# Three gated branches of a transformer block: weights made the moving operand, and the merged sum turned by TensorE

## The chip, the cores and the metric

The program runs on one core of a Trainium2 chip. The metric is the device time of one execution in microseconds (us). TensorE (PE in the profile) multiplies matrices, VectorE is DVE, ScalarE is ACT, and SyncE (SP) issues the DMAs. All engines run their own instruction streams in program order and meet through semaphores.

## The reference, cut to what matters

The first block (256 tokens, 1024 features) ends its mixer with three branches, each a matmul multiplied by a gate of its own:

```
gates = sigmoid(gate_pre)                       # [256 tokens, 3 branches, 1024]
merged = gates[0] * y_conv + gates[1] * y_sb + gates[2] * y_x
# y_conv = conv @ w_conv_out, y_sb = o_sb @ w_sb_out, y_x = o_x @ w_x_out
# gate_pre = h @ w_in[:, 7*1024:10*1024]
x = x + merged @ w_out
h2 = rms_norm(x, g_mlp)
x = x + square(relu(h2 @ w_up)) @ w_down
```

Two further layers follow. All is float32.

## The kernel before, in words

**Weights.** Every weight matrix streams in as "halves" of 1 MB, `[128, 2048]` float32, 4 tiles of 512 columns or 8 of 256. SyncE loads half `l` into `raw[:, l % 2]` once DVE has finished with half `l - 2`. ACT's `split` rounds it to `w_hi` (L331) and DVE's `split` forms the remainder `w_lo = raw - w_hi` (L725); both write slot `l % 4` of a ring of four. A product of float32 precision is three products: hi*hi, lo*hi, hi*lo. In the loop over `h` of the first block (`for h in range(FFN1)`), each engine does what belongs to half `h`, and ACT and DVE then split half `h + 4`, which may begin once PE has finished half `h` (`gemm_done`).

**Two ways to multiply.** `rows_first` (its matmuls are recorded at L1282) holds a 128x128 piece of the weights and moves 256 tokens past it: 48 matmuls of 256 columns for a half, and the result stands feature-first, `[128 features, 256 tokens]` twice in one PSUM bank. `tokens_half` and `tokens_part` (L1321, L1322, L1327) hold 128 tokens of the activation and move 512 weight columns: 24 matmuls of 512 columns for a half, and the result stands token-first, `[128 tokens, 512 features]`, in two banks, one for each `m` of the two token groups. With `tokens_half` a half is only half of the contraction, so two halves (`g` 0 and 1) make up one pair of banks.

**The stage that is changed: halves 36 to 59.** Three branches of eight halves: 36 to 43 the stick-breaking attention ("sb"), 44 to 51 the cross attention ("x"), 52 to 59 the convolution ("conv"). Even halves are gate weights, odd ones the branch's output weights, all by `rows_first`. PSUM `gps` banks 0 to 2 are used in turn; PE starts half `h` when half `h - 3` has been read out (semaphore `evac`). ACT applies the sigmoid to an even half (L557) and copies an odd one to `staged` (L347); DVE multiplies by the gate and adds into `merged` (L1073, L1075, L1077). In the last branch each quarter of `merged` is rounded to `Q_hi` by ACT (L565) and `Q_lo` is formed by DVE (L1083). They are the stationary operand of halves 60 to 63, `merged @ w_out`, by `tokens_part` into the `aps` banks. `square`, norm and MLP follow (halves 64 to 95).

**Beside it.** Cross attention is computed in the same loop iterations, 35 to 40: after the matmuls of a half PE issues `cx_values` (L1490), `cx_transpose` (L1479) and `cx_scores` (L1468) of neighbouring heads, DVE the maximum (L1010, L1013) and scaling (L1018, L1021), ACT the exponential (L511) and copies (L497, L504). The norm of the query heads takes a Ln (L351) and an Exp (L353) on ACT, and its last one (`head_rsqrt(7)`) is due in iteration 36.

Of the kernel before, what the change touches and what calls it, by code (L numbers as in the profile page):

```python
# [14 lines left out]
F32 = mybir.dt.float32  # L15
# [5 lines left out]
P = 128  # L21
D = 1024
# [52 lines left out]
def build(nc, mem_t, x_t, x, w1, w2, wf, rows1, rows2, par1, par2, con1, con2, out):  # L75
    with ExitStack() as ctx:
# [3 lines left out]
        def sem(name):  # L80
# [35 lines left out]
        merged, ox = B1, B3  # L116
# [5 lines left out]
        scaled = B1[:, :, :].rearrange("p a t -> p (a t)").rearrange("p (m n) -> p m n", m=2)  # L122
# [47 lines left out]
            mg mg_hi mg_lo ffn_relu ffn_sq ffn_hi hidden  # L170
# [152 lines left out]
        def _(act):  # L323
# [200 lines left out]
            for h in range(FFN1):  # L524
# [194 lines left out]
        def _(dve):  # L719
# [311 lines left out]
            for h in range(FFN1):  # L1031
# [34 lines left out]
                elif 36 <= h < WO1 and (h - 36) % 2 == 1:  # L1066
                    i = (h - 36) // 2 % 4
                    dve.wait_ge(s["evac"], h + 1)
                    m = merged[:, 2 * i:2 * i + 2, :]
                    sg, gg = staged[:, staged_n % 2, :], gate[:, staged_n % 2, :]  # L1070
                    staged_n += 1
                    if h < GATED["x"]:
                        dve.tensor_tensor(m, two(sg), two(gg), ALU.mult).then_inc(s["staged_free"], 1)  # L1073
                    else:
# [200 lines left out]
        def _(pe):  # L1275
# [221 lines left out]
            for h in range(FFN1):  # L1497
# [14 lines left out]
                elif h < WO1:  # L1512
                    if (h - 36) % 2 == 0:
                        rows_first(0, h, h % 3, H_hi, H_lo)
                    elif h < GATED["x"]:
                        if h == GATED["sb"] + 1:
                            pe.wait_ge(s["sb_olo"], SB_PAIRS)
# [345 lines left out]
```

## Time and profile before

| | |
|---|---|
| median of 3 runs | 1312.22 us (1306.88, 1312.22, 1312.27) |
| the profiled execution | 1308.6 us; its span, first to last instruction, 1306.8 us |
| PE busy | 1245.1 us (95% of the span) |
| PE in the chain that ended last | 75% of the span |
| halves 36 to 59 | 268.29 to 424.60 us of the span |
| halves 60 to 63 | 424.60 to 446.40 us |

Times inside the trace count from the span's start. A row of a timeline is: start, duration, engine, line, operation, what it writes and reads, shapes, how many are merged in the row (xN), and, in square brackets, how long the engine had been idle before it and what ended that. A matmul's duration contains its passage through the array, so the interval between the starts of two matmuls is what each costs in a stream.

### The profile page before, as it was taken

The numbers are of one execution on the slowest core, as the hardware profiler recorded it, in microseconds if no ns is written. First come the engines' busy times: TensorE is split into PE (matmuls) and PEld (weight loads), VectorE is DVE, ScalarE is ACT, GpSimd is POOL, SyncE is SP. The second block draws the span as 40 slices with busy tenths as digits, with TensorE's granted clock in tenths as the row PEclk, the third lists the DMA queues.
The fourth block names the chain that finished last, engine by engine and source line by source line (L and its number), as shares of the span: only waits on it lengthen the run. The fifth ranks groups of instructions, "written<-read, shape, count | busy, mean of one in ns | idle before, by whom it ended". The sixth has DMA issues, their size and how long they took to land.

```text
span 1306.8 us, 19708 instructions
## 1 busy us (share of the span) xinstructions
PE 1245.1 (95%) x8208; PEld 1124.8 (86%) x8208; DVE 775.6 (59%) x823; ACT 616.4 (47%) x676; POOL 0.2 (0%) x4
## 2 busy tenths in 40 slices
PE   5989999999999999999999989999998998899997
PEld 5979998989999899998787868989978886789896
DVE  5566875764555565555356586555566566765545
ACT  4555554664534454444254535544435434454441
POOL 0000000000000000000000000000000000000000
PEclk9989999999999999999999999999999999999999
DMA  6644344433655356554353334655525334365550
GB/s 214 219 158 162 127 164 144 179 125 134 214 203 181 129 212 207 193 183 171 114 202 108 148 139 166 222 181 199 169 94 194 129 129 177 130 209 193 193 193 32
DMA packets 33250, 216.88 MB, mean 166 GB/s; under 512 B 4384, under 2 KB 6432, under 8 KB 7456
## 3 DMA queue, kind: packets, MB, share of 16 engines
q1 hardware_dynamic: 33184, 215.92, 47.5%
q8 instruction: 51, 0.84, 0.3%
q14 instruction: 15, 0.12, 0.0%
HBM read 214.85 MB, written 1.05 MB: 165 GB/s over the span
## 4 chain that ended last, share of the span: by engine, by line
PE 75%; DVE 11%; DMA 6%; ACT 5%; issue 2%; SPq 0%; ACTq 0%; DVEq 0%
PE gps L1282 39%; PE aps L1321 7%; PE aps L1322 7%; PE aps L1327 7%; DMA raw<-w 6%; DVE w_lo L725 4%; PE gps L1321 3%; ACT w_hi L331 3%; PE gps L1322 3%; PE gps L1327 3%; PE aps L1432 1%; DVE B L873 1%; DVE rs L863 1%; DVE B L867 1%; DVE B L817 1%
## 5 line engine op out<-in xcount | busy, mean ns | idle before, releaser
L725 DVE TENSOR_TENSOR w_lo<-raw,w_hi 128x2048 fp32r<-128x2048 f32 x200 | 449.0, 2248 | 288.1 <-ACT w_hi L331 287.8
L331 ACT ACTIVATE w_hi<-raw 128x2048 fp32r<-128x2048 f32 x200 | 374.1, 1875 | 210.9 <-DMA raw<-w 122.1
L1282 PE MATMUL gps<-H_hi,w_hi 128*128 128x256 f32 x896 | 240.9, 290 | 12.5 <-ACT H_hi L366 5.7
L1282 PE MATMUL gps<-H_hi,w_lo 128*128 128x256 f32 x896 | 236.6, 285 | 0.0
L1282 PE MATMUL gps<-R_hi,w_hi 128*128 128x256 f32 x800 | 209.2, 283 | 0.0
L1282 PE MATMUL gps<-R_hi,w_lo 128*128 128x256 f32 x800 | 209.0, 283 | 0.0
L1282 PEld LDWEIGHTS gps<-H_hi,w_hi 128*128 128x128 f32 x896 | 174.1, 194 | 16.4 <-issue 12.9
L1282 PE MATMUL gps<-H_lo,w_hi 128*128 128x256 f32 x896 | 181.4, 285 | 0.0
L1282 PEld LDWEIGHTS gps<-H_hi,w_lo 128*128 128x128 f32 x896 | 174.1, 194 | 0.7 <-issue 0.5
L1321 PE MATMUL aps<-w_hi,Q_hi 128*128 128x512 f32 x416 | 162.2, 390 | 0.8 <-DVE Q_lo L923 0.8
L1322 PE MATMUL aps<-w_lo,Q_hi 128*128 128x512 f32 x416 | 162.1, 390 | 0.0
L1282 PE MATMUL gps<-R_lo,w_hi 128*128 128x256 f32 x800 | 160.5, 283 | 0.0
L1282 PEld LDWEIGHTS gps<-R_hi,w_lo 128*128 128x128 f32 x800 | 153.5, 192 | 0.8
L1282 PEld LDWEIGHTS gps<-R_hi,w_hi 128*128 128x128 f32 x800 | 153.4, 192 | 0.8
L1282 PEld LDWEIGHTS gps<-H_lo,w_hi 128*128 128x128 f32 x896 | 141.1, 194 | 0.0
L1282 PEld LDWEIGHTS gps<-R_lo,w_hi 128*128 128x128 f32 x800 | 124.5, 192 | 0.0
L1327 PE MATMUL aps<-w_hi,Q_lo 128*128 128x512 f32 x416 | 111.2, 389 | 0.0
L1321 PEld LDWEIGHTS aps<-w_hi,Q_hi 128*128 128x128 f32 x416 | 78.2, 188 | 16.5 <-DVE Q_lo L923 1.0
L1327 PEld LDWEIGHTS aps<-w_hi,Q_lo 128*128 128x128 f32 x416 | 78.1, 188 | 16.2
L1322 PEld LDWEIGHTS aps<-w_lo,Q_hi 128*128 128x128 f32 x416 | 78.2, 188 | 15.7
L406 ACT ACTIVATE staged<-gps 128x512 f32<-128x512 f32 x42 | 25.0, 596 | 103.6 <-PE gps L1282 103.6
L347 ACT ACTIVATE B<-gps 128x512 f32<-128x512 f32 x56 | 32.3, 588 | 72.2 <-PE gps L1282 63.3
(223 smaller groups left out, 1377.2 us busy)
## 6 DMA issues: line engine op xcount, KB each, us to landing
raw<-w SPq DMA_DIRECT2D x196, 1024.0 KB, 4.9
B<-rows SPq DMA_DIRECT2D x4, 1024.0 KB, 4.5
B<-x_t SPq DMA_DIRECT2D x2, 512.0 KB, 4.6
B<-mem_t SPq DMA_DIRECT2D x1, 1024.0 KB, 9.1
B<-x SPq DMA_DIRECT2D x1, 1024.0 KB, 7.7
B<-con SPq DMA_DIRECT2D x1, 1024.0 KB, 9.6
out<-B SPq DMA_DIRECT2D x4, 256.0 KB, 2.0
B<-rows SPq DMA_DIRECT2D x1, 512.0 KB, 6.2
```

The costliest lines, as they stand in the source:

```text
L331: act.activation(w_hi[:, ring(l), 0:n], raw[:, raw_slot(l), 0:n], ACT.Copy)\
L347: act.activation(dst, src, ACT.Copy, scale=scale).then_inc(s["evac"], 1)
L406: act.activation(staged[:, a, :], up_bank(par_, a), ACT.Relu)\
L725: dve.tensor_tensor(w_lo[:, ring(l), 0:n], raw[:, raw_slot(l), 0:n], w_hi[:, ring(l), 0:n].bitcast(F32), ALU.subtract)\
L817: ins = dve.scalar_tensor_tensor(t, t, scale, out, ALU.mult, ALU.add)
L863: st.mark(dve.bn_stats(stats[:, m, 6 * j:6 * j + 6], chunk(X, m, j)))
L867: st.mark(dve.scalar_tensor_tensor(t, t, stats[:, m, 12:13], g_row[:, 512 * j:512 * (j + 1)], ALU.subtract, ALU.mult))
L873: dve.scalar_tensor_tensor(t, t, stats[:, m, 17:18], b_row[:, 512 * j:512 * (j + 1)], ALU.mult, ALU.add).then_inc(s["t_z"], 1)
L1282: return pe.matmul(gps[:, bank_, nt * T:(nt + 1) * T], w[:, r, c:c + P], op[:, k, :], start=start, stop=stop, skip_group_check=True)
L1321: pe.matmul(out, x, w_hi[:, r, c], start=(start and k == ks[0]), stop=False)
L1322: pe.matmul(out, x, w_lo[:, r, c], start=False, stop=False)
L1327: ins = pe.matmul(out, op_lo[:, 4 * g + k, rows], w_hi[:, r, c], start=False, stop=(stop and k == ks[-1]))
```

## The change

The 24 halves of the stage are all multiplied token-first. They are ordered in quadruples: two halves make gate columns `512*c` to `512*c + 511` for both token groups, and two make the same columns of the branch. ACT therefore does nothing for a bank in half of the iterations and handles two banks in the others; DVE does its work for a branch once in four. `merged` lies token-first, so it has to be turned before it can be the stationary operand: PE transposes it against the identity (16 transposes of 128x128) into `aps` banks, 8 after the matmuls of half 56 and 4 after each token group's matmuls of half 60, and ACT and DVE make `Q_hi` and `Q_lo` from there. The host packs the weights in another order; their bytes and their number of DMAs stay.

```
-        merged, ox = B1, B3
+        ox = B3
...
+        merged = scaled = B1[:, :, :].rearrange("p a t -> p (a t)").rearrange("p (m n) -> p m n", m=2)
...
@@ ACT
-                    if (h - 36) % 2 == 0:
-
-                        act.wait_ge(s["gemm_done"], h + 1)
-                        act.wait_ge(s["staged_free"], staged_n - 1)
-                        act.activation(gate[:, staged_n % 2, :], ps, ACT.Sigmoid).then_inc(s["evac"], 1)
-                    else:
-                        act.wait_ge(s["staged_free"], staged_n - 1)
-                        evac(staged[:, staged_n % 2, :], ps, h + 1)
-                        staged_n += 1
-                        if h > GATED["conv"]:
-                            i = (h - GATED["conv"]) // 2
-                            act.wait_ge(s["mg"], i + 1)
-                            act.activation(Q_hi[:, 2 * i:2 * i + 2, :], merged[:, 2 * i:2 * i + 2, :],
-                                           ACT.Copy).then_inc(s["mg_hi"], 1)
+                    if (h - 36) % 4 == 1:
+                        for m in range(2):
+                            act.wait_ge(s["gemm_done"], h + 1)
+                            act.wait_ge(s["staged_free"], staged_n + m - 1)
+                            act.activation(gate[:, m, :], bank(h - 1 + m), ACT.Sigmoid).then_inc(s["evac"], 1)
+                    elif (h - 36) % 4 == 3:
+                        for m in range(2):
+                            act.wait_ge(s["staged_free"], staged_n - 1)
+                            evac(staged[:, m, :], bank(h - 1 + m), h + 1)
+                            staged_n += 1
                 elif h == WO1:
                     act.preload_act_table_set("natural_log_exp_and_others")
+                if h in (GATED["conv"] + 4, WO1):
+                    for m in range(2):
+                        j = int(h == WO1)
+                        act.wait_ge(s["mg_tr"], 2 * j + m + 1)
+                        act.activation(operand(Q_hi, m, j), four(turned(m, j)), ACT.Copy)\
+                           .then_inc(s["mg_hi"], 1)
...
@@ DVE
-                elif 36 <= h < WO1 and (h - 36) % 2 == 1:
...
+                elif 36 <= h < WO1 and (h - 36) % 4 == 3:
+                    for m in range(2):
+                        dve.wait_ge(s["evac"], h + m)
+                        t = chunk(merged, m, (h - 36) // 4 % 2)
+                        sg, gg = staged[:, m, :], gate[:, m, :]
+                        staged_n += 1
+                        if h < GATED["x"]:
+                            dve.tensor_tensor(t, sg, gg, ALU.mult).then_inc(s["staged_free"], 1)
+                        else:
+                            st.mark(dve.tensor_tensor(sg, sg, gg, ALU.mult))
+                            st.settle()
+                            dve.tensor_tensor(t, t, sg, ALU.add).then_inc(s["staged_free"], 1)
+                            if h > GATED["conv"]:
+                                dve.wait_ge(s["staged_free"], staged_n)
+                                dve.sem_inc(s["mg"], 1)
+                if h in (GATED["conv"] + 4, WO1):
+                    for m in range(2):
+                        j = int(h == WO1)
+                        dve.wait_ge(s["mg_hi"], 2 * j + m + 1)
+                        dve.tensor_tensor(operand(Q_lo, m, j), four(turned(m, j)),
+                                          operand(Q_hi, m, j).bitcast(F32), ALU.subtract)\
                            .then_inc(s["mg_lo"], 1)
...
@@ PE
+            def turn_merged(j, m):
+
+                pe.wait_ge(s["mg"], 2 * j + m + 1)
+                for k in range(4):
+                    ins = pe.transpose(turned(m, j)[:, k * P:(k + 1) * P],
+                                       chunk(merged, m, j)[:, k * P:(k + 1) * P], ident)
+                ins.then_inc(s["mg_tr"], 1)
...
-                    if (h - 36) % 2 == 0:
-                        rows_first(0, h, h % 3, H_hi, H_lo)
...
+                    g, first = (h - 36) % 2, GATED["conv"] + 2
+                    banks = ((h - g) % 3, (h - g + 1) % 3)
+                    second_free = h - 1 if g == 0 else None
+                    if (h - 36) % 4 < 2:
+                        tokens_half(0, h, g, banks, H_hi, H_lo, second_free)
...
+                    if h == GATED["conv"] + 4:
+                        turn_merged(0, 0)
+                        turn_merged(0, 1)
                 elif h < WO1 + 2:
                     pe.wait_ge(s["lo_ready"], h + 1)
                     for m in range(2):
+                        c = m + 1 if h == WO1 else m + 3
                         ins = tokens_part(h, acc(m, h - WO1), m, 0, Q_hi, Q_lo, start=True,
-                                          hi_ready=(s["mg_hi"], 2), lo_ready=(s["mg_lo"], 2))
-                    ins.then_inc(s["gemm_done"], 1)
+                                          hi_ready=(s["mg_lo"], c))
+                        if m == 1:
+                            ins.then_inc(s["gemm_done"], 1)
+                        if h == WO1:
+                            turn_merged(1, m)
...
@@ host
-        return [x[i:i + 1] for i in range(4) for x in (g, w)]
+        return [value_halves(x[:, c:c + 512]) for c in (0, 512) for x in (g, w)]
```

How the instruction order changes is shown at three places. First ACT in iterations 36 and 37, from the first head's exponential (L511) on. `ACT_TABLE_LOAD` loads the tables of another function; the line beside it is the instruction that needs it (L557 the sigmoid, L351 Ln, L353 Exp, L331 the split of a weight half, L504 and L497 copies out of cross attention). Before:

```order
L511 ACTIVATE B,small<-aps,small 128x256
L557 ACT_TABLE_LOAD [waits staged_free]
L557 ACTIVATE B<-gps 128x512 [waits gemm_done]
L331 ACTIVATE w_hi<-raw 128x2048 [waits gemm_done,raw_loaded0]
L351 ACT_TABLE_LOAD
L351 ACTIVATE rs<-rs 128x256 [waits hn_var]
L353 ACT_TABLE_LOAD
L353 ACTIVATE rs<-rs 128x256 [waits act_step]
L504 ACTIVATE B<-aps 128x512 [waits cx_t]
L511 ACTIVATE B,small<-aps,small 128x256 [waits cx_t,cx_max]
```

The same place of the changed kernel:

```order
L511 ACTIVATE B,small<-aps,small 128x256
L331 ACTIVATE w_hi<-raw 128x2048 [waits gemm_done,raw_loaded0]
L351 ACTIVATE rs<-rs 128x256 [waits hn_var]
L353 ACTIVATE rs<-rs 128x256 [waits act_step]
L504 ACTIVATE B<-aps 128x512 [waits cx_t]
L511 ACTIVATE B,small<-aps,small 128x256 [waits cx_t,cx_max]
L511 ACTIVATE B,small<-aps,small 128x256
L557 ACT_TABLE_LOAD [waits staged_free]
L557 ACTIVATE B<-gps 128x512 [waits gemm_done]
L557 ACTIVATE B<-gps 128x512 [waits staged_free,gemm_done]
```

The sigmoid of iteration 36 has moved behind the second head's exponential, and the three table loads ahead of that exponential are gone.

Second, PE from the last matmuls of half 60's first token group to the start of the second; what reads `w_hi,Q_hi` here is `merged @ w_out`. Before:

```order
L1322 MATMUL aps<-w_lo,Q_hi 128x512
L1327 MATMUL aps<-w_hi,Q_lo 128x512 [waits mg_lo]
L1327 MATMUL aps<-w_hi,Q_lo 128x512 x3
L1321 MATMUL aps<-w_hi,Q_hi 128x512 [waits mg_hi]
L1322 MATMUL aps<-w_lo,Q_hi 128x512
```

The same place of the changed kernel, where the `aps<-cst,B` rows at L1357 are the transposes:

```order
L1326 MATMUL aps<-w_lo,Q_hi 128x512
L1331 MATMUL aps<-w_hi,Q_lo 128x512 x4
L1357 MATMUL aps<-cst,B 128x128 [waits mg]
L1357 MATMUL aps<-cst,B 128x128 x3
L1325 MATMUL aps<-w_hi,Q_hi 128x512 [waits mg_lo]
L1326 MATMUL aps<-w_lo,Q_hi 128x512
```

Four transposes that wait for the last sum stand between the two token groups.

Third, DVE in iterations 59 to 61: the gate product and the sum, the remainder `Q_lo`, and the splits of weight halves (L725). Before:

```order
L1075 TENSOR_TENSOR staged<-staged,B 128x512 [waits evac]
L1077 TENSOR_TENSOR B<-B,staged 128x512 [waits dve_step]
L1083 TENSOR_TENSOR Q_lo<-B,Q_hi 128x512 [waits staged_free,mg_hi]
L725 TENSOR_TENSOR w_lo<-raw,w_hi 128x2048 [waits hi_ready] x3
```

The same place of the changed kernel:

```order
L1077 TENSOR_TENSOR staged<-staged,B 128x512 [waits evac]
L1079 TENSOR_TENSOR B<-B,staged 128x512 [waits dve_step]
L1077 TENSOR_TENSOR staged<-staged,B 128x512 [waits staged_free,evac]
L1079 TENSOR_TENSOR B<-B,staged 128x512 [waits dve_step]
L727 TENSOR_TENSOR w_lo<-raw,w_hi 128x2048 [waits staged_free,hi_ready]
L1087 TENSOR_TENSOR Q_lo<-aps,Q_hi 128x4x128 [waits mg_hi] x2
L727 TENSOR_TENSOR w_lo<-raw,w_hi 128x2048 [waits hi_ready] x2
```

The last `Q_lo` now stands behind a second pair of sums and behind the split of half 63.

## Rows read from the trace of the kernel before

**Rows 1.** The page: span, and busy time, share and instructions of PE.

```profile
span 1306.8 us, 19708 instructions
PE 1245.1 (95%) x8208; PEld 1124.8 (86%) x8208; DVE 775.6 (59%) x823; ACT 616.4 (47%) x676; POOL 0.2 (0%) x4
```

**Rows 2.** The page: shares of the chain that ended last, by engine.

```profile
PE 75%; DVE 11%; DMA 6%; ACT 5%; issue 2%; SPq 0%; ACTq 0%; DVEq 0%
```

**Rows 3.** Busy time by stretch: halves 42 to 59, then 60 to 63.

```profile
320.90:424.60 103.70, 103.70 (x866) 103.70 (x865) 56.63 (x41) 47.61 (x43) 0.00 (x0) 1.00 0.56 195
424.60:446.40 21.80, 21.80 (x99) 17.98 (x98) 12.84 (x15) 9.89 (x12) 0.00 (x0) 1.00 0.57 193
```

**Rows 4.** Timeline of PE: first matmuls of halves 42 and 60, what follows 63.

```profile
320.92 0.28 PE L1282 MATMUL gps<-H_hi,w_hi 128*128 128x256 f32 x1
...
424.60 0.40 PE L1321 MATMUL aps<-w_hi,Q_hi 128*128 128x512 f32 x1
...
446.40 1.04 PE L1345 MATMUL aps<-cst,B 128*128 128x128 f32 x8
```

**Rows 5.** Timeline of PE: token-first half 30, rows-first half 32, float32 products between.

```profile
227.44 0.58 PE L1321 MATMUL gps<-w_hi,R_hi 128*128 128x512 f32 x1
...
233.11 1.02 PE L1458 MATMUL gps<-sqh,cst 128*128 128x256 f32 x4
...
240.13 0.47 PE L1282 MATMUL gps<-H_hi,w_hi 128*128 128x256 f32 x1
...
246.07 1.02 PE L1458 MATMUL gps<-sqh,cst 128*128 128x256 f32 x4
```

**Rows 6.** Timeline of PE: cross attention behind halves 36 and 37.

```profile
276.52 0.66 PE L1479 MATMUL aps<-cst,B 128*128 128x128 f32 x4 [1.27 <-DVE B L1021]
...
284.50 1.89 PE L1490 MATMUL aps<-B 128*128 128x256 f32 x8
287.92 0.66 PE L1479 MATMUL aps<-cst,B 128*128 128x128 f32 x4 [1.53 <-DVE B L1021]
```

**Rows 7.** Timeline of ACT and DVE in iteration 36.

```profile
275.63 1.28 ACT L557 ACT_TABLE_LOAD   x1
...
278.58 0.42 DVE L734 TENSOR_SCALAR rs<-gps 128x256 f32<-128x256 f32 x1
...
279.34 1.28 ACT L351 ACT_TABLE_LOAD   x1
...
281.07 1.28 ACT L353 ACT_TABLE_LOAD   x1
...
282.89 0.43 DVE L742 SCALAR_TENSOR_TENSOR rs<-rs 128x256 f32<-128x256 f32 x1 [3.89 <-ACT rs L353]
```

**Rows 8.** Timeline of PE: eight transposes in the MLP, and the matmul behind them.

```profile
466.02 1.04 PE L1402 MATMUL gps<-cst,spb 128*128 128x128 f32 x8
466.81 0.36 PE L1282 MATMUL gps<-R_hi,w_hi 128*128 128x256 f32 x1
```

**Rows 9.** The page: the two splits of a weight half, mean ns of one.

```profile
L725 DVE TENSOR_TENSOR w_lo<-raw,w_hi 128x2048 fp32r<-128x2048 f32 x200 | 449.0, 2248 | 288.1 <-ACT w_hi L331 287.8
L331 ACT ACTIVATE w_hi<-raw 128x2048 fp32r<-128x2048 f32 x200 | 374.1, 1875 | 210.9 <-DMA raw<-w 122.1
```

**Rows 10.** Timeline of ACT and DVE from the end of half 59.

```profile
424.86 0.60 ACT L347 ACTIVATE staged<-gps 128x512 f32<-128x512 f32 x1 [3.42 <-PE gps L1282]
...
425.49 0.69 DVE L1075 TENSOR_TENSOR staged<-staged,B 128x512 f32<-128x512 f32 x1 [1.73 <-ACT staged L347]
...
426.22 0.69 DVE L1077 TENSOR_TENSOR B<-B,staged 128x512 f32<-128x512 f32 x1
...
427.00 0.63 ACT L565 ACTIVATE Q_hi<-B 128x512 fp32r<-128x512 f32 x1 [1.54 <-DVEq L1081]
...
429.45 1.28 ACT L568 ACT_TABLE_LOAD   x1
```

**Rows 11.** Timeline around half 10, token-first: a late weight DMA and a bank.

```profile
81.02 1.91 ACT L331 ACTIVATE w_hi<-raw 128x2048 fp32r<-128x2048 f32 x1 [5.52 <-DMA raw<-w]
...
83.47 0.80 PE L1321 MATMUL gps<-w_hi,H_hi 128*128 128x512 f32 x1 [3.52 <-ACT B L347]
```

**Rows 12.** The page: the weight DMAs, KB each, median us to landing.

```profile
raw<-w SPq DMA_DIRECT2D x196, 1024.0 KB, 4.9
```

More of the change, by code:

```diff
@@ L169, in build @@
             cx_s cx_max cx_exp cx_p cx_t cx_pt cx_o cx_oe ox_hi ox_lo
[L170 removed]
+            mg mg_tr mg_hi mg_lo ffn_relu ffn_sq ffn_hi hidden
             f_pick f_sp f_decay f_dhi f_dlo fx_s fx_l fx_max fx_e fx_p fx_t fx_pt fx_o fx_ohi fx_oe
@@ L1065, in _ @@
                         dve.tensor_tensor(t, t, sg, ALU.mult).then_inc(s["staged_free"], 1)
-                elif 36 <= h < WO1 and (h - 36) % 2 == 1:
[L1067 to L1074, printed above, removed]
-                        st.mark(dve.tensor_tensor(sg, sg, gg, ALU.mult))
-                        st.settle()
-                        dve.tensor_tensor(m, m, two(sg), ALU.add).then_inc(s["staged_free"], 1)
-                    if h > GATED["conv"]:
-                        dve.wait_ge(s["staged_free"], staged_n)
-                        dve.sem_inc(s["mg"], 1)
-                        dve.wait_ge(s["mg_hi"], i + 1)
-                        dve.tensor_tensor(Q_lo[:, 2 * i:2 * i + 2, :], m,
-                                          Q_hi[:, 2 * i:2 * i + 2, :].bitcast(F32), ALU.subtract)\
+                elif 36 <= h < WO1 and (h - 36) % 4 == 3:
[13 more added lines that the diff above has]
+                                dve.sem_inc(s["mg"], 1)
@@ L1512, in _ @@
                 elif h < WO1:
-                    if (h - 36) % 2 == 0:
-                        rows_first(0, h, h % 3, H_hi, H_lo)
-                    elif h < GATED["x"]:
-                        if h == GATED["sb"] + 1:
-                            pe.wait_ge(s["sb_olo"], SB_PAIRS)
-                        rows_first(0, h, h % 3, Q_hi, Q_lo)
-                    elif h < GATED["conv"]:
-                        rows_first(0, h, h % 3, Q_hi, Q_lo, (s["ox_hi"], s["ox_lo"], 0, (1, 2, 3, 4)) if h == GATED["x"] + 1 else None)
+                    g, first = (h - 36) % 2, GATED["conv"] + 2
[3 more added lines that the diff above has]
+                        tokens_half(0, h, g, banks, H_hi, H_lo, second_free)
+                    elif h < GATED["conv"]:
+                        if h == GATED["sb"] + 2:
+                            pe.wait_ge(s["sb_olo"], SB_PAIRS)
+                        if h == GATED["x"] + 2:
+                            pe.wait_ge(s["ox_lo"], 2)
+                        if h == GATED["x"] + 3:
+                            pe.wait_ge(s["ox_lo"], 4)
+                        tokens_half(0, h, g, banks, Q_hi, Q_lo, second_free)
                     else:
-                        if h == GATED["conv"] + 1:
+                        if h == first:
                             pe.wait_ge(s["cv_lo"], 4)
-                        rows_first(0, h, h % 3, R_hi, R_lo)
+                        tokens_half(0, h, g, banks, R_hi, R_lo, second_free)
+                    if h == GATED["conv"] + 4:
+                        turn_merged(0, 0)
+                        turn_merged(0, 1)
                 elif h < WO1 + 2:
@@ L1817, in pairs @@
     def pairs(g, w):
-        return [x[i:i + 1] for i in range(4) for x in (g, w)]
+        return [value_halves(x[:, c:c + 512]) for c in (0, 512) for x in (g, w)]
     win, kv = a["w_in"][0], a["w_mem_kv"][0]
-    col = [halves(win[:, i * D:(i + 1) * D]) for i in range(10)]
-    c_h, c_b, c_c, sq, sk, sv, xq, g0, g1, g2 = col
+    col = [halves(win[:, i * D:(i + 1) * D]) for i in range(7)]
+    c_h, c_b, c_c, sq, sk, sv, xq = col
+    g0, g1, g2 = (win[:, i * D:(i + 1) * D] for i in (7, 8, 9))
     w1 = np.concatenate(
@@ L1825 @@
          value_halves(kv[:, D:]), xq]
-        + pairs(g1, halves(a["w_sb_out"][0])) + pairs(g2, halves(a["w_x_out"][0]))
-        + pairs(g0, halves(a["w_conv_out"][0])) + [deep_halves(a["w_out"][0])]
+        + pairs(g1, a["w_sb_out"][0]) + pairs(g2, a["w_x_out"][0])
+        + pairs(g0, a["w_conv_out"][0]) + [deep_halves(a["w_out"][0])]
         + mlp_order(a["w_up"][0], a["w_down"][0]))
```

3 lines of the change are left out of this document (1 added, 2 removed).

## The prediction

> **What bounds the kernel now.** I read the page first: PE is busy 95% of the span of 1306.8 us [rows 1] and is 75% of the chain that ended last [rows 2]. Then the busy time by stretch: over halves 42 to 59 PE is busy for all of 103.70 us at a granted clock of 1.00, which is the 2.4 GHz level, while ACT has 47.61 and DVE 56.63 us of work; the weight loads fill the stretch as well [rows 3]. So from half 42 on no wait reaches PE, and the stage costs what its matmuls cost. Third, PE's timeline shows where halves 36 to 41 differ: two waits for cross attention, 1.27 us ahead of the transpose at 276.52 and 1.53 us ahead of the one at 287.92, both on DVE's scaling [rows 6]. Those two are the only idle time that PE has between 268 and 446 us. A microsecond of PE saved here is therefore a microsecond of the span, unless a new wait takes it.
>
> **The pace of a half.** From the first matmul of half 42 (320.92) to that of half 60 (424.60) are 18 rows-first halves: 103.68 / 18 = 5.76 us, or 120.0 ns for each of 48 matmuls. Halves 60 to 63 are token-first: (446.40 - 424.60) / 4 = 5.45 us, or 227.1 ns for each of 24 [rows 4]. 256 more columns cost 107.1 ns, so some 13 ns of every matmul does not depend on its columns, and half as many matmuls save 24 x 13 ns = 0.31 us a half. Behind float32 products both kinds are slower: token-first 233.11 - 227.44 = 5.67 us, rows-first 246.07 - 240.13 = 5.94 us [rows 5], a difference of 0.27 us. Halves 37 to 41 start behind such products, 42 to 59 do not: 5 x 0.27 + 18 x 0.31 = 6.9 us. Half 36 gives nothing: the transpose at 276.52 waits for DVE, whose chain does not contain half 36, so the wait grows by what the half shrinks.
>
> The Trainium skill speaks against this term ("TensorE: Matmul & The Clock Gate", section "Wait — 56ns, not 53.3ns?"): a warm matmul costs its columns at 2.4 GHz and a fixed 2.5 ns. By that a half would save 24 x 2.5 ns = 0.06 us and 23 halves 1.4 us. These rows show five times that fixed part, and I go by them.
>
> **The wait at 287.92.** In iteration 36 ACT loads three tables, 1.28 us each: for the sigmoid of half 36, for the Ln and for the Exp of the last query norm [rows 7]. In the changed order the sigmoids come in iteration 37, behind the second head's exponential, and none of the three loads stands ahead of it. The Ln needs the variance that DVE writes at 278.58 to 279.0, so it can start at about 279.0 instead of 280.6; without the load in between, Exp ends at about 279.9 and DVE's step at 282.89 moves to about 280.0, 2.9 us earlier. All that follows (norm, maximum, exponential, scaling) moves with it, and the second transpose's operand is there at 287.9 - 2.9 = 285.0. PE now comes to that transpose at about 286.1: `cx_values` starts at 284.2 (284.50 less 0.3) and holds PE for about 1.9 us [rows 6]. The wait of 1.53 us goes, with 1.1 us to spare. In iteration 37 ACT has both sigmoids, a split, two copies, one table load and the third exponential, together some 7 us from the end of half 37, to about 291.9; the transpose behind half 38 comes at about 295.6. Covered.
>
> **The transposes.** Eight in the MLP take 466.81 - 466.02 = 0.79 us, and the first matmul behind them is 0.08 us longer than usual (0.36 against 0.28) [rows 8]. 16 in three groups: 0.87 for the eight behind half 56, and about 0.5 each for the two groups of four in half 60, 1.85 us in all. Bounds: 1.6 (no switching cost at all) and 2.7 (three groups at the 1.37 us per eight that lie between 446.40 and the next product, a wait included, with the fours dearer). The nearest row is the stream of [rows 8].
>
> **The end of the stage.** Let t be the start of half 60. ACT's first copy starts at t + 0.26, DVE's product at 0.89, its sum at 1.62, and the result is known at t + 2.4 [rows 10]. The first group of transposes comes after 12 matmuls, at t + 2.75: just covered. The second token group's product and sum follow at once and end near 3.9; its transposes come at about 6.0. On DVE the split of half 63 is next: 3.95 to 6.2, by 2.25 us for one [rows 9]. ACT meanwhile: copies to 1.4, split to 3.3, the table load of 1.28 us [rows 10] to 4.6, `Q_hi` for the first token group to 5.2. So `Q_lo` runs from 6.2 to 6.9, and PE, which would start half 61 at about t + 6.4 (5.45 + 0.5 + 0.5), waits 0.5 us. Queued behind that wait are all of halves 61 to 63. Bounds: 0, if the split of 63 is quicker by what the copies save, and 2, if it is held by a late raw load. The second token group's `Q_lo` ends near 8.1 and is needed at 9.7. The MLP norm starts from the last products as before. The turn behind half 56 is covered: its sums end by 4 us into a half of 5.45.
>
> **Costed at nothing.** Two bank reads in a row: ACT's first is done 0.9 us after the pair, PE wants the bank in the middle of the next half, 2.7 us after; cover 1.8 us. The splits: a half is split at the latest 6.2 us after the half four before it ended (1.1 copies or 2.9 DVE work, 1.9, 2.3), and is needed 16 us after. The raw slot is then free for a DMA of 4.9 us [rows 12], there at 11.1, when ACT asks at 10.9 plus its copies. PE's run is shorter, the 1 MB per half is not: 4.9 against 5.45 us. ACT, DVE and DMA keep their amount of work.
>
> **Sum.** 6.9 + 1.5 - 1.85 - 0.5 = 6.1 us. Against the profiled execution: its span goes from 1306.8 to 1300.7, its time from 1308.6 to 1302.5. The median shown is 3.6 us above that execution, and from it the sum gives 1306.1. The runs stand at 1307 and at 1312, so I take the middle of both results, 1304.
>
> **Rivals.**
> *More is won* (0.15): no wait at half 61, transposes at 1.6, and some 0.5 us from later waits that move: 6.9 + 1.5 - 1.6 + 0.5 = 7.3 us, 1301.3 from the profiled time. For it speaks that the estimate at half 61 hangs on the order of two items on DVE; against it, that every row says DVE is in order.
> *The turn lies bare* (0.13): the chain from the last bank read to `Q_lo` passes through ACT, DVE, PE, ACT and DVE, where before the last quarter had two further halves of cover. If it is 2 to 3 us longer than above, the gain is 3.5 us and the time 1305 to 1309. The Trainium skill's figure for a transpose in a kernel (same page, section "Part 4: PE-mode transpose", about 275 ns) would make 16 of them 4.4 us and leave 3.6 us too; the rows show about 100 ns each.
> *The pace does not pay* (0.05): the fixed part of a matmul belongs to what PE holds and not to the count. If halves into the `gps` banks ran at 5.70 instead of 5.45, the stage would save 1.4 us, and the sum would be 1.4 + 1.5 - 1.85 - 0.5 = 0.6 us: 1308.0. This is also where the Trainium skill's fixed 2.5 ns leads. Against it: [rows 5] have a `gps` half at 5.67 with the float32 start in it.
> *Slower, by banks* (0.05): at half 10 a raw load that came 5.52 us late held ACT's split, the copy queued behind it came late, and PE idled 3.52 us for a bank [rows 11]. The changed stage has 11 such places. To pass 0.5% slower it must give back the 6.1 us and lose 6.5 more, 1.15 us at each of the 11, for which ACT must be 1.8 + 1.15 = 3.0 us late every time: 1308.6 - 6.1 + 12.6 = 1315. ACT stands idle on PE for 3.42 us ahead of a copy now [rows 10], and that is used up first: it decides only if raw loads come 3.4 + 3.0 = 6.4 us late every time.
>
> **How the numbers follow.** The forecast has 0.62, the others 0.15, 0.13, 0.05 and 0.05. About what a measurement of this kernel tells from no change is 0.5%, 6.5 us, and the forecast of 6.1 lies just under it: with its own range of 5.3 to 6.9 us I give 0.27 of its 0.62 to faster. Faster: 0.27 + 0.15 = 0.42. Same: 0.35 + 0.13 + 0.05 = 0.53. Slower: 0.05. The range goes from the larger gain on the lower runs, 1306.9 - 7.3 = 1299.6, to the smaller gain on the upper ones, 1312.2 - 3.5 = 1308.7: 1299.5 to 1309.
>
> **What the profile would show.** Right: token-first halves of 5.45 us between half 42 and 56; no wait ahead of the transpose behind half 37, with 1.6 us left ahead of the first; three table loads fewer on ACT; 16 transposes in under 2 us; a wait of about 0.5 us on `Q_lo` at half 61; halves 36 to 59 over in some 148.7 us instead of 156.3 (6.9 + 1.5 - 0.9 for the eight transposes less). Wrong: halves above 5.6, PE idle for a bank read, or a wait above 1 us at half 61.

## The result, and the profile after

The changed kernel takes 1299.58 us (median of 5 runs, 1295.43 to 1301.07), the one before beside it 1309.53 us (5 runs). The ratio is 0.9917 with a 95% interval of 0.9892 to 0.9942: faster by 10 us, and clearly more than the 0.5% that the prediction drew as its line. The forecast was 1304.0 with a gain of 6.1 us, and more chance on "no change that can be told" than on "faster".

The page of the changed kernel, the lines that answer to [rows 1]:

```profile
span 1298.7 us, 18585 instructions
PE 1242.6 (96%) x7648; PEld 1098.8 (85%) x7648; DVE 775.8 (60%) x823; ACT 612.7 (47%) x673; POOL 0.2 (0%) x4
```

PE's busy time fell by only 2.5 us and the span by 8.1. From half 36 to the transposes of the norm it fell by 5.6 us, from 175.31 to 169.71. Behind that, where both programs do the same, it rose by 4.0 us, from 820.26 to 824.24, at a mean granted clock of 0.98 instead of 0.99; in the second pair of traces, shown below, it did not (822.08 and 821.21). So busy time summed over the span is no measure of this change. The starts tell it. PE's timeline of the changed kernel through the changed stage, from halves 36 and 37 to the transposes of the norm:

```profile
266.29 0.58 PE L1325 MATMUL gps<-w_hi,H_hi 128*128 128x512 f32 x1
273.91 0.66 PE L1491 MATMUL aps<-cst,B 128*128 128x128 f32 x4 [0.94 <-DVE B L1023]
275.95 0.58 PE L1325 MATMUL gps<-w_hi,H_hi 128*128 128x512 f32 x1
281.61 1.89 PE L1502 MATMUL aps<-B 128*128 128x256 f32 x8
283.34 0.60 PE L1491 MATMUL aps<-cst,B 128*128 128x128 f32 x4
...
315.17 0.39 PE L1325 MATMUL gps<-w_hi,Q_hi 128*128 128x512 f32 x1
...
396.77 1.03 PE L1357 MATMUL aps<-cst,B 128*128 128x128 f32 x8
397.56 0.48 PE L1325 MATMUL gps<-w_hi,H_hi 128*128 128x512 f32 x1
...
413.98 0.39 PE L1325 MATMUL aps<-w_hi,Q_hi 128*128 128x512 f32 x1
416.71 0.60 PE L1357 MATMUL aps<-cst,B 128*128 128x128 f32 x4
417.06 0.48 PE L1325 MATMUL aps<-w_hi,Q_hi 128*128 128x512 f32 x1
...
419.92 0.60 PE L1357 MATMUL aps<-cst,B 128*128 128x128 f32 x4
421.04 0.47 PE L1325 MATMUL aps<-w_hi,Q_hi 128*128 128x512 f32 x1 [0.52 <-DVE Q_lo L1087]
...
437.47 0.60 PE L1349 MATMUL aps<-cst,B 128*128 128x128 f32 x4
```

To be seen: one wait of 0.94 us is left of the two in [rows 6]; the second transpose (283.34) starts without one. From 315.17 to 396.77 are 15 halves, 5.44 us each, against 5.76 before. Eight transposes move the next matmul from 396.77 to 397.56, 0.79 us, the first four in half 60 from 416.71 to 417.06, 0.35 us. The wait on `Q_lo` at half 61 is 0.52 us by its bracket. Half 36 starts at 266.29, so halves 36 to 59 take 147.69 us (before: 156.31, by [rows 4] and the start of half 36), and halves 60 to 63 take 437.47 - 413.98 = 23.49 (before: 21.80). Together 171.18 against 178.11 us: **the stage gives 6.93 us**, where 6.1 were forecast.

Two windows of it, pure token-first halves and halves 60 to 63 (stretch, length, busy time and instructions of PE, PEld, DVE, ACT and POOL, granted clock, DMA share, GB/s), against [rows 3]:

```profile
315.10:396.80 81.70, 81.70 (x363) 67.58 (x362) 45.19 (x33) 38.97 (x35) 0.00 (x0) 1.00 0.58 209
414.00:437.40 23.40, 22.88 (x105) 18.77 (x104) 14.93 (x18) 10.95 (x14) 0.00 (x0) 1.00 0.52 180
```

PE is still busy for all of the first stretch, at the 2.4 GHz level; 0.52 us of the second is idle. ACT and DVE show why the second wait at cross attention is gone. Both in iteration 36 of the changed kernel, the places of [rows 7]:

```profile
275.97 0.42 DVE L736 TENSOR_SCALAR rs<-gps 128x256 f32<-128x256 f32 x1
276.43 0.42 ACT L351 ACTIVATE rs<-rs 128x256 f32<-128x256 f32 x1 [1.62 <-DVE rs L736]
276.88 0.42 ACT L353 ACTIVATE rs<-rs 128x256 f32<-128x256 f32 x1
277.40 0.42 DVE L744 SCALAR_TENSOR_TENSOR rs<-rs 128x256 f32<-128x256 f32 x1 [1.01 <-ACT rs L353]
281.54 1.28 ACT L557 ACT_TABLE_LOAD   x1
```

Ln and Exp follow the variance at once, with no table load between, and the load for the sigmoid comes only at 281.54. Counted from the start of half 36, DVE's step at L744 is at 11.1 us instead of 14.6.

So 6.9 us come from the stage. The other 1.2 us of the difference in span are outside it: half 36 starts 2.0 us earlier, where both programs are still the same, and what follows the stage takes 0.8 us longer.

### The profile page after: what moved, and what is told of

It is laid out like the page before. It is cut to its first block, busy times and chain, and to the rows that moved or that the text cites. A ratio compares the mean times of both kernels' runs of the same rounds, so it can differ in the third digit from the quotient of the medians.

```text
span 1298.7 us, 18585 instructions
## 1 busy us (share of the span) xinstructions
PE 1242.6 (96%) x7648; PEld 1098.8 (85%) x7648; DVE 775.8 (60%) x823; ACT 612.7 (47%) x673; POOL 0.2 (0%) x4
## 4 chain that ended last, share of the span: by engine, by line
PE 78%; DVE 11%; DMA 5%; ACT 4%; issue 2%; SPq 0%; DVEq 0%; ACTq 0%
PE gps L1286 32%; PE aps L1325 7%; PE aps L1326 7%; PE aps L1331 7%; PE gps L1325 6%; PE gps L1326 6%; PE gps L1331 6%; DMA raw<-w 5%; DVE w_lo L727 4%; ACT w_hi L331 2%; PE aps L1444 1%; DVE B L875 1%; DVE rs L865 1%; PE aps L1648 1%; DVE B L869 1%
## 5 line engine op out<-in xcount | busy, mean ns | idle before, releaser
L331 ACT ACTIVATE w_hi<-raw 128x2048 fp32r<-128x2048 f32 x200 | 374.4, 1876 | 231.5 <-DMA raw<-w 130.8
L1286 PE MATMUL gps<-H_hi,w_hi 128*128 128x256 f32 x704 | 190.6, 292 | 12.5 <-ACT H_hi L366 5.7
L1286 PE MATMUL gps<-R_hi,w_hi 128*128 128x256 f32 x736 | 192.5, 283 | 0.0
L1286 PE MATMUL gps<-R_hi,w_lo 128*128 128x256 f32 x736 | 192.3, 283 | 0.0
L1286 PE MATMUL gps<-H_hi,w_lo 128*128 128x256 f32 x704 | 186.8, 286 | 0.0
L1286 PEld LDWEIGHTS gps<-H_hi,w_hi 128*128 128x128 f32 x704 | 137.3, 195 | 16.1 <-issue 12.8
L1286 PE MATMUL gps<-H_lo,w_hi 128*128 128x256 f32 x704 | 142.8, 286 | 0.0
L1286 PEld LDWEIGHTS gps<-H_hi,w_lo 128*128 128x128 f32 x704 | 137.6, 196 | 0.6 <-issue 0.5
L1286 PEld LDWEIGHTS gps<-H_lo,w_hi 128*128 128x128 f32 x704 | 111.3, 195 | 0.0
L1325 PE MATMUL gps<-w_hi,H_hi 128*128 128x512 f32 x192 | 79.3, 413 | 3.2 <-ACT B L347 2.2
L1326 PE MATMUL gps<-w_lo,H_hi 128*128 128x512 f32 x192 | 76.2, 397 | 0.0
```

Source lines behind the costliest of these rows:

```text
L331: act.activation(w_hi[:, ring(l), 0:n], raw[:, raw_slot(l), 0:n], ACT.Copy)\
L1286: return pe.matmul(gps[:, bank_, nt * T:(nt + 1) * T], w[:, r, c:c + P], op[:, k, :], start=start, stop=stop, skip_group_check=True)
L1325: pe.matmul(out, x, w_hi[:, r, c], start=(start and k == ks[0]), stop=False)
L1326: pe.matmul(out, x, w_lo[:, r, c], start=False, stop=False)
```

## The experiments

### Both kernels once more

To see how far one trace stands for its kernel, both were run again, unchanged.

> The kernel before, unchanged, timed against itself. It tells how far two medians of one program lie apart. Theory A (the change is worth what its stage shows, 6.9 us between the starts of the last half before it and of the norm behind it, and the other 3 us of the measured 10 are scatter that both programs have): the medians may differ by up to 3 us, and the trace shows idle time of PE of other lengths than before at the late raw loads (half 10 among them). Theory B (the change makes the rest of the program faster too): the medians lie within 1 us, so that 10 us cannot be scatter.

> The changed kernel, unchanged, timed against before a second time. Theory A: the gain is 7 us with a scatter of 3, so 4 to 10. Theory B: it is 10 to 11 us again. In both the trace has the same stage: halves 36 to 59 in about 147.7 us, halves 60 to 63 in about 23.5 us.

Measured: 1309.1 us (ratio 1.0, 0.9988 to 1.0012) and 1298.05 us (0.9918, 0.99 to 0.9936). The lead is there again, 8.4 to 13.1 us. The kernel before came out 0.3 us from the median of 1308.8 us beside which it was timed, so a lead of 10 us is not scatter between two medians. PE in the new trace of the kernel before:

```profile
266.20 0.47 PE L1282 MATMUL gps<-H_hi,w_hi 128*128 128x256 f32 x1
273.89 0.66 PE L1479 MATMUL aps<-cst,B 128*128 128x128 f32 x4 [0.73 <-DVE B L1021]
285.28 0.55 PE L1479 MATMUL aps<-cst,B 128*128 128x128 f32 x3 [1.52 <-DVE B L1021]
421.97 0.40 PE L1321 MATMUL aps<-w_hi,Q_hi 128*128 128x512 f32 x1
443.77 0.49 PE L1345 MATMUL aps<-cst,B 128*128 128x128 f32 x3
```

Stage: 177.57 us, against 171.08 in the changed kernel's second trace, 6.5 us. The second wait is the same to 0.01 us. The first is 0.73 us here and 1.27 in [rows 6]: the chain ahead of it scatters by half a microsecond, and the prediction started from a long one. Half 36 starts 2.1 us earlier than in the first trace of the same kernel. **The stage repeats to 0.5 us, what stands ahead of it only to 2.** The gain in time is 11.1 us by these medians (10.7 by the ratio), the gain in the stage 6.5.

### One part at a time

The edits below are cut to what matters.

**The pace alone** (`narrow`): the changed kernel, with each matmul of halves 36 to 59 cut in two.

```diff
-ins = pe.matmul(bank, x, w[..., 512*k:512*(k+1)])
+for n in range(2):
+    ins = pe.matmul(bank[:, 256*n:256*(n+1)], x, w[..., 512*k + 256*n:512*k + 256*(n+1)])
```

> The changed kernel, with each 512-column matmul of halves 36 to 59 split into two of 256 columns on the same stationary tile; all else as changed. If the pace is a matter of the number of matmuls (13 ns each, as the prediction had it), each half takes 5.76 us again and the gain over before falls by 24 x 0.31 = 7.4 us, to about 0 by the traces. If the pace comes from which operand is held (token-first, fewer different tiles), halves stay near 5.45 us and the gain stays.

Measured: 1308.07 us, ratio 1.0 (0.9985 to 1.0015). PE at the same places as above:

```profile
403.53 1.04 PE L1384 MATMUL aps<-cst,B 128*128 128x128 f32 x8
404.32 0.48 PE L1342 MATMUL gps<-w_hi,H_hi 128*128 128x256 f32 x2
...
421.67 0.40 PE L1325 MATMUL aps<-w_hi,Q_hi 128*128 128x512 f32 x1
```

Halves 57 to 59 take (421.67 - 404.32) / 3 = 5.78 us, in the changed kernel (413.98 - 397.56) / 3 = 5.47. The difference is the forecast 0.31 us per 24 matmuls saved. Halves 36 to 59 take 154.74 us, 7.1 more, and 23 x 0.31 = 7.1. The same operand sits still in both, so it is the number of matmuls that costs, not what PE holds: this settles the rival "the pace does not pay". Each added matmul comes with a weight load of its own (the page counts 8224 of both, 7648 in the changed kernel), and no run tells which of the two costs the 13 ns. By the Trainium skill ("TensorE: Matmul & The Clock Gate", section "Wait — 56ns, not 53.3ns?") the fixed part is about 2.5 ns, and the cut would have cost 1.4 us by an estimate from that figure; here it is 13 ns, with a weight load beside every matmul. With halves 60 to 63 at 23.51 the stage is 178.25 us, that of the kernel before within 0.7, and the whole time is equal too: the turn, its wait and the removed waits cancel.

**The table loads alone** (`before_sig`): the kernel before, with the sigmoid of half 36 moved behind the exponential in iteration 37. **And put back** (`after_tables`): the changed kernel with a sigmoid over its own gate buffer in iteration 36, which leads to the same three loads.

```diff
 # before_sig, ACT
 if (h - 36) % 2 == 0:
-    sigmoid(h)
+    if h > 36:
+        sigmoid(h)
 else:
+    if h == 37:
+        sigmoid(36)
```

```diff
 # after_tables, ACT
+if h == 36:
+    act.wait_ge(s["gemm_done"], h + 1)
+    act.activation(gate[:, 1, :], gate[:, 1, :], ACT.Sigmoid)
```

> The kernel before, with one part of the change alone: the sigmoid of half 36 is done in iteration 37 and so behind the second head's exponential. The prediction's step: the wait of 1.53 us behind half 37 goes and the one of 1.27 us behind half 36 stays; halves 36 to 59 take 156.3 - 1.5 = 154.8 us. Rival: the first wait shrinks as well, as in the changed kernel (0.94 us), and the stage loses 2.1 us. Second rival: the loads were hidden, and nothing changes.

> The changed kernel with one more sigmoid (on a gate buffer that is written anew afterwards) in iteration 36, where the old order had it, so that three table loads stand ahead of the second head's exponential again. By the prediction's step the second wait comes back: the operand of the transpose is 3.8 us later, at 11.0 us after the first transpose instead of 7.2 to 8.4, and PE idles 1.5 to 2.0 us there. If the wait was not the tables', nothing comes back.

PE's two cross-attention transposes in `before_sig`:

```profile
275.63 0.55 PE L1484 MATMUL aps<-cst,B 128*128 128x128 f32 x3 [0.78 <-DVE B L1026]
285.33 0.60 PE L1484 MATMUL aps<-cst,B 128*128 128x128 f32 x4
```

and in `after_tables`:

```profile
273.56 0.66 PE L1494 MATMUL aps<-cst,B 128*128 128x128 f32 x4 [0.79 <-DVE B L1026]
...
285.00 0.66 PE L1494 MATMUL aps<-cst,B 128*128 128x128 f32 x4 [1.85 <-DVE B L1026]
```

Moving one sigmoid takes the second wait away, and bringing it back restores it, at 1.85 us. Halves 36 to 59: 154.07 us in `before_sig` (1.7 and 2.2 less than in the two traces of before), 149.62 in `after_tables` (1.9 to 2.0 more than in those of after). The cause of the wait is shown both ways. The first wait is 0.78 us in `before_sig`, as good as the 0.73 in `before_again`: the sigmoid has no part in it. In time, `after_tables` is 1300.89 us, 2.8 above `after_again`, though the intervals of their ratios just overlap (0.993 to 0.9965 and 0.99 to 0.9936); `before_sig` is 1307.37, ratio 0.9994 (0.998 to 1.0008), which neither shows nor excludes 1.7 us.

**Twice the transposes** (`after_turn2`):

```diff
-for k in range(4):
+for k in (0, 1, 2, 3, 0, 1, 2, 3):
     ins = pe.transpose(turned(m, j)[:, k * P:(k + 1) * P], ...
```

> The changed kernel with each of the 16 transposes issued twice, so the price of 16 transposes by itself. By the stream row 16 x 0.10 = 1.6 us more (0.8 behind half 56, 0.4 in each of the two groups of half 60), part of the last two hidden in the wait of 0.5 us on Q_lo. By a price of about 275 ns for one it would be 4.4 us.

PE in `after_turn2`:

```profile
395.19 1.91 PE L1357 MATMUL aps<-cst,B 128*128 128x128 f32 x16
396.86 0.48 PE L1325 MATMUL gps<-w_hi,H_hi 128*128 128x512 f32 x1
419.63 1.03 PE L1357 MATMUL aps<-cst,B 128*128 128x128 f32 x8
420.42 0.48 PE L1325 MATMUL aps<-w_hi,Q_hi 128*128 128x512 f32 x1
```

16 take 1.67 us where 8 took 0.79, 0.11 us for each one added, and a group of eight in half 60 takes 0.79. The 0.52 us wait at half 61 is filled by the added transposes: halves 60 to 63 take 23.57 us, 0.08 more. The time, 1297.59 us, shows none of the 1.1 us that the trace shows for the stage. The Trainium skill states about 275 ns for a transpose in a kernel (same page, section "Part 4: PE-mode transpose"). The trace agrees for the duration of one, 272 ns, but in a stream they overlap and start 0.11 us apart, so that this figure is not what each of them costs here.

**Without the wait at half 61** (`after_early`): DVE forms the first token group's `Q_lo` ahead of the split of half 63, and ACT preloads its table behind the copies to `Q_hi`.

```diff
 # DVE: merged_lo(m, 1) waits for Q_hi and forms Q_lo
+if h == WO1 - 1:
+    merged_lo(0, 1)        # ahead of this iteration's split
 if h == WO1:
-    merged_lo(0, 1)
     merged_lo(1, 1)
 # ACT
-elif h == WO1:
-    act.preload_act_table_set("natural_log_exp_and_others")
 ... the two copies to Q_hi ...
+if h == WO1:
+    act.preload_act_table_set("natural_log_exp_and_others")
```

> The changed kernel, with two things moved at the end of the stage: DVE forms the first token group's last Q_lo ahead of the split of half 63 instead of behind it, and ACT loads the tables for Ln and Exp behind both Q_hi copies instead of ahead. By the prediction's step the first group's Q_lo is then ready at about 4.9 us after half 60 starts, PE's wait of 0.52 us at half 61 goes and halves 60 to 63 take 23.0 us instead of 23.5. If the wait were for something else (the turn's own length), it stays.

PE, ACT and DVE in the changed kernel around the wait, behind the start of half 60 at 413.98:

```profile
417.15 1.28 ACT L564 ACT_TABLE_LOAD   x1
418.00 2.29 DVE L727 TENSOR_TENSOR w_lo<-raw,w_hi 128x2048 fp32r<-128x2048 f32 x1
418.45 0.60 ACT L569 ACTIVATE Q_hi<-aps 128x512 fp32r<-128x512 f32 x1
420.21 0.68 DVE L1087 TENSOR_TENSOR Q_lo<-aps,Q_hi 128x512 fp32r<-128x512 f32 x1
```

and in `after_early`, behind a start at 414.86:

```profile
418.22 0.60 ACT L567 ACTIVATE Q_hi<-aps 128x512 fp32r<-128x512 f32 x1 [0.22 <-PE aps L1363]
418.88 0.69 DVE L1085 TENSOR_TENSOR Q_lo<-aps,Q_hi 128x512 fp32r<-128x512 f32 x1
419.49 2.28 DVE L727 TENSOR_TENSOR w_lo<-raw,w_hi 128x2048 fp32r<-128x2048 f32 x1
...
420.80 0.60 PE L1363 MATMUL aps<-cst,B 128*128 128x128 f32 x4
421.15 0.47 PE L1331 MATMUL aps<-w_hi,Q_hi 128*128 128x512 f32 x1
```

`Q_lo` starts 4.0 us after half 60 instead of 6.2, the matmul at 421.15 has no wait in its row, and halves 60 to 63 take 22.73 us, 0.75 less. The time is 1297.61 us (1295.94 to 1300.83) against 1298.05: better in the trace, and within the scatter of the whole time, so that nothing can be said of the time.

### Where do the other microseconds come from?

The lead is 10 to 11 us and the stage explains 6.5 to 6.9. In the expectations, theory A is scatter, and B says that the change makes the rest of the program faster too. B could work in four ways: late raw loads outside the stage happen to fall differently; the token-first work itself saves more in time than its trace shows; PE's instruction fetches, of which the page of the kernel before counts 51 and that of the changed one 47, stand beside the weight loads at other moments (theory C); or what comes later runs at other moments against the loads (theory D). Each was tried on a pair, since the scatter of one trace hides it.

**Half the weight bytes** (both kernels, twice; PE multiplies old numbers in the rest), so that loads come earlier:

```diff
-sp.dma_start(raw[:, a, :], w1[...])
+sp.dma_start(raw[:, a, 0:HALF // 2], w1[...][:, 0:HALF // 2])
```

> The kernel before, but the loops' weight DMAs bring the first 1024 of each partition's 2048 columns, so half the bytes; ACT and DVE still split all 2048 and PE multiplies them, with old numbers in the rest, so the result is not the reference's. Raw loads can then not be late. Both theories: the idle time at half 10 (3.52 us) goes, and the span is some 5 to 15 us under 1306.8. It is the base for the next run.

> The changed kernel with the same light weight DMAs (half the bytes; the result is not the reference's). Theory A: without late loads the spans of the two light kernels differ by the stage alone, 6.5 to 7.3 us, and by nothing before half 36 or after half 63. Theory B, if the rest gains through PE or the instruction stream: 9 to 11 us. If B works through the weight DMAs (fewer collisions), 7 us here and 10 with full loads.

> The kernel before with the light weight DMAs again (half the bytes; the result is not the reference's), in more rounds: 1291 to 1293 if the first median was a fair one.

> The changed kernel with the light weight DMAs again (half the bytes; the result is not the reference's). With it the light pair's difference is known to about 1 us. If what is gained outside the stage needs late weight loads, the difference is the stage's 6.3 us (5.5 to 7.2); if not, 9 to 10 us.

**128 semaphore increments ahead of PE's first wait** (both):

```diff
+for _ in range(128):
+    pe.sem_inc(s["shift"], 1)
 pe.wait_ge(s["par_loaded"], 32)
```

> The kernel before, with 128 semaphore increments ahead of PE's first wait, where PE idles 9.5 us anyway: no work is changed, but all of PE's code stands further along, so that its 16 KB instruction fetches fall at other moments beside the weight DMAs. Theory C (the 3 us that the change gains outside its stage come from the instruction fetches, of which it needs 47 instead of 51 and at other moments): the time moves by 1.5 us or more, in either direction, and the idle times of PE in the first layer's mixer (0.8, 0.9 us at late splits) with it. Theory A (scatter of late loads and of the granted clock, in which program position plays no part): within 1 us of before.

> The changed kernel with the same 128 increments at the start. Theory C: its lead of 10 us over before changes by 1.5 us or more. Theory A: it stays at 10 to 11 us.

**16 more float32 products in the stage** (both):

```diff
+if h in (46, 48, 50, 52):
+    for _ in range(4):
+        pe.matmul(aps[:, 1, :], ident, cst[:, 0:512], start=True, stop=True)
```

> The kernel before with the same 16 products. Theories A and C: it rises by what its stage rises, about 7 us, to 1316. Theory D: by another amount, 4 to 10 us, since its later parts run at other moments too.

> The changed kernel with 16 float32 products (identity times 512 constant columns, into an aps bank that nothing reads then) behind the matmuls of halves 46, 48, 50 and 52: about 7 us more of PE in the stage with 16 more instructions of code. Theory D (the 3 us outside the stage depend on when the later parts run): the time rises by the 7 us of the stage and by 3 more, to about 1308. Theory C (they depend on how much code there is and where it stands): it rises by what the stage rises, to about 1305. Theory A: also 1305.

Medians, and the stage from half 36 to the norm's transposes as one trace of each shows it (sums of starts, as above):

| pair | before | after | gain in time | gain in the stage |
|---|---|---|---|---|
| unchanged, first | 1309.53 | 1299.58 | 9.9 | 6.9 |
| unchanged, again | 1309.1 | 1298.05 | 11.1 | 6.5 |
| half the bytes, first | 1291.84 | 1286.16 | 5.7 | 6.3 |
| half the bytes, second | 1293.24 | 1285.9 | 7.3 | 6.3 |
| increments | 1315.25 | 1308.09 | 7.2 | 6.5 |
| longer stage | 1319.38 | 1312.16 | 7.2 | 6.4 |

The stage's gain is the same in all six, 6.3 to 6.9 us. The altered pairs win about what their stage wins; the unchanged pair wins 3 to 4 us more. Three other kernels with the token-first stage and full bytes have a surplus too, beside the kernel before: 4.0 us in `after_early`, 4.8 in `after_turn2`, 2.4 in `after_tables` (gain of the medians less gain of the stage, against the 177.57 us of `before_again`).

With half the bytes the gain is 5.7 and 7.3 us, where 7 was expected if the surplus came through the weight loads and 9 to 11 otherwise. This speaks against the token-first work itself: in the altered pairs the same work gives no surplus. `narrow` speaks against a surplus that sits in the changed order of ACT and DVE, or in the turn: it has both, its stage is as long as before's, and so is its time.

The increments took 11.0 us (the first matmul starts at 20.49 instead of 9.5) and weren't hidden as intended, and the products took 13.8 us in the stage instead of 7, so both are larger disturbances than planned. They cost the two kernels different amounts: the increments 6.6 us in the kernel before and 10.0 in the changed one, the products 10.9 and 14.1. So by the medians it is the kernel before that gets 3 to 4 us back when it is disturbed. Late loads that happen to fall differently, C and D would all do that, and these two pairs can't tell them apart. The interval of each ratio reaches 0.0012 to 0.0025 to either side, 1.6 to 3.3 us, so that 7.2 and 10.7 are not sharply apart.

The traces show where the surplus stands. Over the six traces of kernels that have the token-first stage with full bytes and no increments, all that is outside it takes 1125.7 us in the mean (1122.9 to 1128.5), over the five with 48 matmuls a half 1129.1 (1126.8 to 1130.8). 1.3 us of this difference stands ahead of half 36 and 2.1 behind the stage, where the two programs do the same. Behind the stage PE idles 28.9 us in the mean of the six (28.2 to 29.9) and 31.7 in that of the five (29.9 to 32.6). The difference is in its waits for two results of DVE in the MLP and the two further layers, `spb` and `Q_lo`: 1.3 us in the mean (0.4 to 2.3) against 4.2 (3.1 to 5.3). In all four traces with half the bytes PE has no such wait. One of them in `narrow`, ACT's split and then PE:

```profile
666.15 1.91 ACT L331 ACTIVATE w_hi<-raw 128x2048 fp32r<-128x2048 f32 x1 [2.50 <-DMA raw<-w]
675.74 0.88 PE L1653 MATMUL aps<-cst,spb 128*128 128x128 f32 x6 [1.85 <-DVE spb L1175]
```

and the same place of the changed kernel:

```profile
656.55 1.91 ACT L331 ACTIVATE w_hi<-raw 128x2048 fp32r<-128x2048 f32 x1 [1.29 <-DMA raw<-w]
666.14 0.88 PE L1626 MATMUL aps<-cst,spb 128*128 128x128 f32 x6 [0.52 <-DVE spb L1175]
```

ACT waits for the raw load, DVE for ACT's split, and the chain of `spb` stands behind that split in DVE's program order: 1.2 us more of waiting for the load are 1.3 us more of idle PE. So in these traces the part of the surplus that stands behind the stage is waiting for late weight loads. **Why they come later for PE in kernels with 48 matmuls a half stays open.** C is neither shown nor excluded: the nine traces with the token-first stage count 47 instruction fetches, the eight others 51 or 52, `narrow` among them, and no run changes that count alone. Fetches by themselves don't make the surplus, since with half the bytes the counts are 51 and 47 too.

## Why the prediction was partly right

- **Pace.** Right: 5.44 us for a half (forecast 5.45), 281.61 - 275.95 = 5.66 behind float32 products (5.67). `narrow` shows that it is a price per matmul, and takes back 7.1 us of 6.9 forecast.
- **The wait at 287.92.** Right: gone in the changed kernel, gone in `before_sig`, back at 1.85 us in `after_tables`. ACT loads 11 tables instead of 14 in the whole trace, three fewer, as forecast.
- **The first wait.** The prediction let it grow by 0.3 us from 1.27. It is 0.79 to 1.10 in the seven token-first traces with full bytes, 0.73 to 0.80 in four further ones of the old order, and 0.57 in `narrow`, whose half 36 is as long as before's. Growth of 0.1 to 0.2 us over the four; the term was right in kind, its base a long draw. This is most of the 0.8 us by which the stage gave more than the sum.
- **Transposes.** 0.79 us for the eight (forecast 0.87) and 0.35 for a four (forecast 0.5; 0.35 also in `after_early`, 420.80 to 421.15): 1.5 us for the 16 instead of 1.85. The 4.4 us of the rival took the duration of one (272 ns here) for its price in a stream.
- **The wait at half 61.** Forecast 0.5, measured 0.52, and the order in which it arises is the one forecast: `Q_lo` starts at t + 6.23, forecast t + 6.2. `after_early` removes it, and its 0.75 us say that such an idle time costs more in starts than its bracket shows: 421.04 - 419.92 is 1.12, 0.77 more than the four alone, because the bracket counts only from the transposes' end.
- **Halves 36 to 59** in 147.69 us, forecast 148.7; halves 60 to 63 longer by 1.69, forecast 1.5.
- **Banks and raw loads.** PE is idle for neither in the stage. The rivals "the turn lies bare", "the pace does not pay" and "slower, by banks" are out. "More is won" gave 7.3 us, the nearest to the 6.9 of the stage, for one of its reasons: the transposes are below even its 1.6, but the wait at half 61 is there. Its "later waits that move" were 0.5 us; the traces show more of them, and outside the stage.

The step that failed is "a microsecond of PE saved here is therefore a microsecond of the span", and with it the step from the sum to the chances. The sum of the stage was taken for the whole difference, with an own range of 5.3 to 6.9 us; what stands outside the stage was put at nothing. The sum lay 0.4 us under the line of 6.5 us, and the larger part of the chance went below. In fact the stage alone gave 6.5 to 6.9, at the line, and the kernels differed by 3 to 4 us more outside it, of which the traces show 2 to 3 us in PE's waits behind late weight loads. Nothing in the profile of before priced that; but its runs at 1306.88 and 1312.27 said that the kernel moves by 5 us with no change at all, and a forecast that hangs on 0.4 us should have carried this scatter of the rest into its range and split its chance evenly at best. That the time of 1299.58 us still lies in the range of 1299.5 to 1309 is luck: its lower end is the stage's largest gain taken from the lowest run, and nothing in it stands for the surplus.

## What to carry to other kernels

Where PE is the bound, count matmuls as well as columns: read the fixed price from two kinds of stream in the same trace (here 13 ns for each matmul with its weight load), and prefer the order that moves 512 columns, even if the result must then be turned. A stage read from starts of the same instruction repeats to half a microsecond and can be forecast term by term; the difference of two whole programs also contains what late loads do elsewhere (here 3 to 4 us), so test a gain near the noise by undoing one part (`narrow`) and not by the total alone. A table load is worth moving only where it stands in the chain that PE waits for: one sigmoid moved removed the whole 1.5 us wait. Two orders with the same amount of work for the loads can still differ in how late the loads reach PE, far from the change: sum PE's waits by what ended them on both sides of it.

## What the runs showed of the hardware

A late raw load costs more than its wait. After the 3.52 us of idle time at half 10 [rows 11] the kernel before ran on at a lower clock. Its windows (columns as above):

```profile
76.00:83.00 7.00, 3.95 (x18) 2.94 (x16) 1.86 (x2) 1.98 (x2) 0.00 (x0) 0.97 0.81 286
83.00:90.00 7.00, 6.53 (x20) 4.75 (x20) 4.55 (x2) 2.81 (x3) 0.00 (x0) 0.54 0.48 160
```

and PE inside the second:

```profile
84.49 0.63 PE L1321 MATMUL gps<-w_hi,H_hi 128*128 128x512 f32 x1
84.92 0.63 PE L1322 MATMUL gps<-w_lo,H_hi 128*128 128x512 f32 x1
```

A granted clock of 0.54 in the mean, and matmuls 0.43 us apart instead of 0.227: the 1.2 GHz level for most of the window. In `after_turn2` the wait in that place is 1.67 us:

```profile
82.48 0.50 PE L1325 MATMUL gps<-w_hi,H_hi 128*128 128x512 f32 x1 [1.67 <-ACT B L347]
```

Its second window, and then that of `before_light`, which has no wait there:

```profile
83.00:90.00 7.00, 7.00 (x35) 5.49 (x35) 4.45 (x3) 4.59 (x5) 0.00 (x0) 1.00 0.60 213
```

```profile
83.00:90.00 7.00, 7.00 (x40) 5.88 (x37) 4.13 (x6) 5.12 (x6) 0.00 (x0) 1.00 0.31 100
```

PE issued 20, 35 and 40 recorded matmuls in the second window of the three, and half 36 starts at 268.29, 264.56 and 261.76 us. Over the eleven traces of kernels with the full bytes and no increments half 36 starts at 264.56 to 268.29 us; waits of this kind are in it, whichever kernel it is.

Two prices: 128 semaphore increments on PE took 20.49 - 9.5 = 11.0 us (the first matmul's start with them and without), 86 ns each, and a float32 product of 128x512, in groups of four and with the change to it and back, took 13.8 / 16 = 0.86 us. Half the weight bytes are worth 15 to 18 us to the kernel before (ratios 0.986 and 0.9883) and some 12 to the changed one (1298.05 to 1286.16 and 1285.9), though in the stage itself PE waits for no late load in either.
